# Down products of two feed-forward parts, each split into two products of 256 columns

## What is computed

```
# block 1: dense feed-forward, 2048 -> 8192 -> 2048
h2 = rmsnorm(x, g_mlp)
u  = relu(h2 @ w_up)              # (256, 8192)
x  = x + (u * u) @ w_down         # (8192, 2048)  <- down products

# block 2: 8 heads x 16 of 16384 experts for each token
h  = h + mix @ w_out
xn = rmsnorm(h)
expert, gate = top16 of the product keys, softmax
hid = gelu(sum_d u_tab[expert, d] * xn[d])
h  = h + sum over experts of gate * hid * v_tab[expert]   # <- down products
```

## Time and profile before

| | |
|---|---|
| runs | 3317.15, 3318.09, 3322.59 us |
| median of the runs | 3318.09 us |
| profiled execution, span | 3316.7 us |
| profiled execution's own time against the median | 1.4 us less by its span; no other figure is given for it |
| matmuls | 20,054, with as many weight loads |
| TensorE busy | 98% of the span |
| VectorE, ScalarE, GpSimd busy | 61%, 44%, 15% |

### The profile page before, as it was taken

How to read it: one execution, slowest core, us unless ns; L and a number is a source line. 1 busy time by engine, 2 the same in 40 slices (tenths; PEclk the granted TensorE clock), 3 DMA queues, 4 the chain that set the end, 5 groups by cost and what they waited for, 6 DMA issues and landing times.

```text
span 3316.7 us, 48331 instructions
## 1 busy us (share of the span) xinstructions
PE 3251.2 (98%) x20054; PEld 2896.3 (87%) x20054; DVE 2039.7 (61%) x1849; ACT 1459.5 (44%) x1268; POOL 486.7 (15%) x418
## 2 busy tenths in 40 slices
PE   7999999999999989999999999999999999999998
PEld 6788899999999878888879999999999888888886
DVE  4455565555555557665456888999874555455554
ACT  5564453344333464453334444455543333333333
POOL 0000000000000002135200002888840000000000
PEclk9999999999999999999999999999999999999999
DMA  6444465555555443342245565676676666556563
GB/s 255 141 164 165 154 229 191 191 191 194 193 193 190 141 164 127 130 150 89 90 164 217 194 223 216 213 247 234 230 252 239 231 236 251 221 224 253 231 237 114
DMA packets 131396, 644.18 MB, mean 194 GB/s; under 512 B 14640, under 2 KB 47664, under 8 KB 61872
## 3 DMA queue, kind: packets, MB, share of 16 engines
q1 hardware_dynamic: 96016, 624.18, 52.4%
q10 hardware_dynamic: 35232, 17.83, 1.8%
HBM read 606.31 MB, written 35.66 MB: 194 GB/s over the span
## 4 chain that ended last, share of the span: by engine, by line
PE 92%; DVE 3%; ACT 2%; DMA 1%; issue 1%; SPq 0%; DVEq 0%; ACTq 0%
PE pj L288 12%; PE pj L289 12%; PE pj L287 12%; PE pj L275 7%; PE pj L274 7%; PE pj L273 7%; PE pj L1637 3%; PE pj L1639 3%; PE pj L1638 3%; PE pj L818 3%; PE pj L820 3%; PE pj L819 3%; PE pm L273 2%; PE pt L273 2%; PE pt L274 2%; PE pm L275 2%
## 5 line engine op out<-in xcount | busy, mean ns | idle before, releaser
L255 ACT ACTIVATE hi<-raw 128x2048 fp32r<-128x2048 f32 x535 | 1025.0, 1916 | 1419.2 <-PE pj L289 661.5
L262 DVE TENSOR_TENSOR lo<-raw,hi 128x2048 fp32r<-128x2048 f32 x400 | 917.1, 2293 | 714.3 <-ACT hi L255 713.7
L287 PE MATMUL pj<-xh,hi 128*128 128x256 f32 x3328 | 927.0, 279 | 0.0
L289 PE MATMUL pj<-xh,lo 128*128 128x256 f32 x3328 | 926.1, 278 | 0.0
L288 PE MATMUL pj<-xl,hi 128*128 128x256 f32 x3328 | 926.0, 278 | 0.0
L287 PEld LDWEIGHTS pj<-xh,hi 128*128 128x128 f32 x3328 | 630.8, 190 | 0.6
L288 PEld LDWEIGHTS pj<-xl,hi 128*128 128x128 f32 x3328 | 625.0, 188 | 0.6
L289 PEld LDWEIGHTS pj<-xh,lo 128*128 128x128 f32 x3328 | 624.8, 188 | 0.0
L262 DVE TENSOR_TENSOR lo_in<-raw,hi 128x2048 fp32r<-128x2048 f32 x135 | 311.4, 2310 | 281.3 <-ACT hi L255 280.7
L2314 POOL TENSOR_SCALAR hotA<-cst,slotT 128x128 fp32r<-128x128 f32 x256 | 328.2, 1297 | 496.2 <-ACT slotT L2157 435.8
L1637 PE MATMUL pj<-hi,xh 128*128 128x512 f32 x576 | 235.7, 409 | 13.4 <-ACT proj L1706 7.3
(11 more groups left out here) (382 smaller groups left out, 4269.8 us busy)
## 6 DMA issues: line engine op xcount, KB each, us to landing
raw<-w_peer SPq DMA_DIRECT2D x256, 1024.0 KB, 6.1
raw<-w_mlp SPq DMA_DIRECT2D x128, 1024.0 KB, 4.9
raw<-w_in SPq DMA_DIRECT2D x104, 1024.0 KB, 4.9
raw<-w_out SPq DMA_DIRECT2D x32, 1024.0 KB, 4.8
raw<-w_q SPq DMA_DIRECT2D x16, 1024.0 KB, 5.0
act_scratch<-hidU SPq DMA_DIRECT2D x32, 512.0 KB, 3.1
gates_scratch<-stage ACTq DMA_DIRECT2D x8, 2048.0 KB, 16.9
hidV<-act_scratch SPq DMA_DIRECT2D x32, 512.0 KB, 3.7
```

The source lines that it names most:

```text
L255: nc.scalar.activation(hi[:, j, :], raw[:, j, :], ACT.Copy).then_inc(hi_ready, 1)
L262: nc.vector.tensor_tensor(low(q)[:, j, :], raw[:, j, :], hi[:, j, :].bitcast(F32), ALU.subtract).then_inc(lo_ready, 1)
L287: nc.tensor.matmul(o, hi[:, j, cols], xh[:, k0 + k, :], start=clears, stop=False, skip_group_check=True)
L289: mm = nc.tensor.matmul(o, lo[:, j, cols], xh[:, k0 + k, :], start=False, stop=end and b % 2 == 1, skip_group_check=True)
```

## The change

Each of the three matmuls of a down product becomes two, over columns 0 to 255 and 256 to 511 of the same moving operand and of the same PSUM bank, with the same stationary. `start` is now given only with the first half of the first product into a bank, `stop` with the last half of the last.

```diff
             for k in range(4):
-                cols = slice(k * NB, (k + 1) * NB)
                 for t in range(TT):
                     tok = slice(t * P, (t + 1) * P)
                     begin, end = first and k == 0, last and k == 3
-                    nc.tensor.matmul(pair[:, t, :], sh[:, k0 + k, tok], hi[:, j, cols], start=begin, stop=False)
-                    nc.tensor.matmul(pair[:, t, :], sh[:, k0 + k, tok], lo[:, j, cols], start=False, stop=False)
-                    mm = nc.tensor.matmul(pair[:, t, :], sl[:, k0 + k, tok], hi[:, j, cols], start=False, stop=end)
+                    for x_, w_ in ((sh, hi), (sh, lo), (sl, hi)):
+                        for half in range(2):
+                            out = slice(half * 256, half * 256 + 256)
+                            cols = slice(k * NB + half * 256, k * NB + half * 256 + 256)
+                            clears = begin and half == 0 and x_ is sh and w_ is hi
+                            mm = nc.tensor.matmul(pair[:, t, out], x_[:, k0 + k, tok], w_[:, j, cols], start=clears,
+                                                  stop=end and half == 1 and x_ is sl, skip_group_check=True)
             mm.then_inc(pe_used, 1)
```

## The result

The changed kernel's median is 3336.58 us (3331.06 to 3339.69, 4 runs) against 3320.34 us of before (3317.15 to 3324.32, 4 runs): a ratio of 1.0048, with a 95% interval of 1.0036 to 1.0061. It is slower, by about 0.5%. The time lies inside the stated range of 3290 to 3350 us, but that range was drawn to take in the rivals. The forecast of no change beyond 0.2% did not come in; one of the rivals did, in part. The profiled execution has a span of 3329.3 us against 3316.7, so 12.6 us more.

A forecast was written before the change was run, and what follows sets the result against it. TensorE's matmul pace was taken to bound the kernel: −3.4 (feed-forward splits) − 0.4 (turns) + 6.8 (expert splits) = +3.0 us on the 3316.7 us span, 3319.7; runs' median 1.4 us higher, so 3321.1 us. Range 3290 to 3350 us.

The forecast's parts named there:

- forecast of no change beyond 0.2%: Whole kernel: both paces stay as now, 3321.1 us or +0.09%, own range 3316 to 3325; chance 0.45.
- What bounds the kernel: Feed-forward part and experts' up and down stages: PE busy throughout, so the pace of the matmuls is the time.
- Counts and weight loads: TensorE: 4,608 matmuls more, on top of 20,054, and as many loads; nothing saves the second load.
- The experts' down stage, +6.8 us: Second block's expert part: 3,072 splits at the slow pace, +2.2 ns each, +6.8 us.
- Block 1's part, −3.4 us and −0.4 us for the turns: Feed-forward part: 1,536 splits at the quick pace, −2.2 ns each; 15 down-to-up turns save 0.03 us each.
- a start-to-start of 117.8 ns before 1133 us: Feed-forward part: this spacing of matmul starts would prove the forecast of 113.3 ns wrong in that stage.
- the slow pace takes hold in the feed-forward part: Rival: slow from the first down quad, at 488 us, and stays; +17 us (3335) or +29 (3347); chance 0.18.
- a triple of 0.35 us after 500 us: Feed-forward up products, lines 290 to 292 of the changed kernel: this length would decide for the slow-pace rival there.
- the down stage leaves the slow pace: Rival, experts' down stage: turns quick, −20.6 us, total 3294; chance 0.24, with quick gates too (3275) 0.04.
- A fixed cost of each added matmul: Rival: 2.2 ns per added matmul in the feed-forward part too, +3.4 for −3.4, so +10: 3328; chance 0.05.
- The loop's return: Rival: instruction fetch shows as idle time at 6 and 14 loop returns, 0 to +62 us; chance 0.04.
- the cases slower by more than 0.2%: Whole kernel: slow pace in the feed-forward part, fixed cost and loop returns together; chance 0.27.

The follow-up runs named there:

- e3: Against the kernel before: halves in the experts' down stage alone, block 1's products whole; 3325.24 us, ratio 1.0018.
- e5: Against the changed kernel: in block 1 the last three products of every down quad stay whole; 3325.3 us, ratio 1.0016 to the kernel before.
- e10: e5 plus three unused whole products ahead of the experts' up quad 27, after the last gate group; 3292.68 us, ratio 0.9916 to the kernel before.
- e11: The kernel before, down products whole, plus three unused whole products ahead of the experts' up quad 27; 3305.76 us, ratio 0.9952.
- e6: The changed kernel plus small groups of unused matmuls between up chunks of the experts' quads 27 to 31; one execution, 3309.56 us.
- e8: e5 plus whole first three experts' down products and three unused ones ahead of quad 27; a reused variable reran four gate groups; 3327.67 us, ratio 1.0020.
- e12: e10 with the other 512-column products, the input and output products of both blocks, also as halves; 3317.47 us, ratio 0.9977 to the kernel before.

## Why the prediction was wrong, and where it was right

**What bounds the kernel: right.** PE has no gap in the three stages in any of these kernels, and every difference between them is one of its pace.

**Counts and weight loads: right.** 4,608 more of each, none saved.

**The experts' down stage, +6.8 us: right.** +6.9 us, in the profiles of before and after and again in e3. The slow pace that the gate groups leave behind persisted over the turn, as it did before.

**Block 1's part, −3.4 us and −0.4 us for the turns: this is the step that failed**, as "feed-forward part, quick pace: 2 x 113.3 − 228.9 = −2.2 ns". The price of a half at the quick pace was right: −2.2 ns for 1,488 split products is −3.3 us, and e5 and e10 have −2.9 us in this part, with 90 halves at its end at the slow pace (+0.4). The stage of 3,072 splits shows it more plainly, at 6.7 us (e10 against e11). What was wrong is that the quick pace would stay. I had read the earlier trace rows, where a turn from 512 to 256 columns takes five slower products and settles at the quick pace, as a small cost that equal shapes would save. It was what kept the part quick: e5 puts that turn back and takes 11.7 us off. The part as it is has 7 of its blocks at the slow pace: 7 x (192 up x 4.4 ns + 96 split products x 8.9 ns) = 11.9 us. With −3.4 for the halves and +0.4 for the last 96 of them this makes +8.9, and +8.8 was measured. The prediction's own sign, a start-to-start of 117.8 ns before 1133 us, came in. Its sum also counts 15 turns from down to up where the trace has 14; the term stays at −0.4.

**The rival "the slow pace takes hold in the feed-forward part"** came true in part: +15.7 us for both parts against its +29 and +17. That the median of 3336.6 is close to its 3335 is luck: 3335 stood for all down products slow and all up products quick, and what happened is about half of both slow. Its place was wrong. It named the first down quad at 488 us, and that quad is quick; the flip comes 20 us later at the turn to up. Its test, a triple of 0.35 us after 500 us, is what the profile shows at 508 us. It also said that a slow pace once entered would stay; it left again at each second turn.

**The rival "the down stage leaves the slow pace"** did not happen in the changed kernel. e6 and e10 show that its price was right (−20.4 us measured, −20.6 forecast) and that it needs the quick pace at the entry.

**A fixed cost of each added matmul: no.** At the quick pace 3,072 more matmuls make the stage 6.7 us shorter (e10 against e11); at the slow pace they make it 6.9 us longer. The Trainium skill ("TensorE: Matmul & The Clock Gate", Back-to-back issue gap) has N/2.4 + 2.5 ns at full clock, and calls it the gap of isolated single matmuls. These traces have about such a surcharge for an added matmul, 2.2 ns, at the slow pace only, and the measurement decides.

**The loop's return: no.** No idle time at any of the 20 returns.

**The chances.** The forecast of the same had 0.45 and the cases slower by more than 0.2% had 0.27. The persistence of the pace was a pattern from one execution over turns of another kind than the change makes, and deserved less than it got.

## What to carry to other kernels

Where a stream of matmuls bounds the time, take the distance between starts, not the busy mean, and look at it stage by stage: at an unchanged granted clock it can have more than one steady value for the same shape. Before removing an irregularity at a boundary (a change of shape, a few slower matmuls), ask what state it leaves behind for the stream that follows. An experiment with small groups of extra work at several places of one stream costs one run and can show a gain that no edit of the real work had pointed at; then measure the kernel that rests on it.

## What the runs showed of the hardware that was not expected

- Float32r streams with one weight load to each matmul have two steady paces at a granted clock of 1.00: 113.3 and 117.8 ns a start for 256 columns, 228.9 and 233.3 ns for 512. Either can persist for 700 us.
- At the quick pace, two halves of 256 columns are 2.2 ns cheaper than one product of 512; at the slow pace they are 2.2 ns dearer.
- What flips the pace: a group of four gate products always left it slow. A turn from down halves to up products, or a single transpose, flipped it either way. Eight transposes left it slow or quick: from slow to quick at 449 us before the change, from quick to slow at 1141 us in the changed kernel, unchanged twice in e6. Three products of 512 columns followed by up products always left it quick, also in the six places of e6 and e8 to e12 where they met the slow pace. Three followed by down halves did not.
- What the state is, and why one order of loads and matmuls flips it and another not, stays open. No run here looks inside TensorE's queue, and the profile's ends of matmuls are modelled.
